# A mixer's depthwise convolution kept in PSUM, PE's units in two pairs of banks, and GpSimd's trailing means moved behind weight splits

## The chip, the cores and the metric

One core of one Trainium2 chip. The metric is the device time of one execution in microseconds (us). The kernel before took 3724.12 us (median of 3 runs, 3720.81 to 3726.64). Its profiled execution took 3723.6 us.

The engines are named as in the profile: PE (TensorE), DVE (VectorE), ACT (ScalarE), POOL (GpSimd), SP (SyncE, which issues the weights' transfers).

## What is computed

A first block (a mixer of gated delta rule and neighbourhood attention, then 16 experts), and behind it a second block of two layers over L = 528 tokens (16 meta tokens and 512) of 1024 features, all in float32. The change touches the second block's mixer alone:

```python
def token_mix(h, w_in, pool_w, pool_scale, conv_dw, conv_db, conv_ln_g, conv_ln_b, conv_pw, ret_gn_g, w_out):
    z = h @ w_in
    xp, ca, cg, q, k, v, g = jnp.split(z, splits, axis=-1)
    y_pool = pool_mixer(xp, pool_w, pool_scale)
    y_conv = conv_module(ca, cg, conv_dw, conv_db, conv_ln_g, conv_ln_b, conv_pw)
    y_ret = retention(q, k, v, g, ret_gn_g)
    return jnp.concatenate([y_pool, y_conv, y_ret], axis=-1) @ w_out

def conv_module(a, gate, w_dw, b_dw, ln_g, ln_b, w_pw):
    u = a * jax.nn.sigmoid(gate)
    y = lax.conv_general_dilated(u, w_dw[:, None, :], window_strides=(1,),
                                 padding=[(CONV_WIDTH - 1, 0)],
                                 dimension_numbers=('NWC', 'WIO', 'NWC'),
                                 feature_group_count=D_CONV) + b_dw
    y = jax.nn.silu(layer_norm(y, ln_g, ln_b))
    return y @ w_pw
```

The convolution has 31 taps over 256 channels (two tiles of 128). `pool_mixer` subtracts each token from trailing means over 2, 4, 8 and 16 tokens and multiplies by a matrix. `retention` rotates q and k (rope), forms decayed scores and values for 4 heads, normalises and gates them. Each layer is: a feed-forward network (FFN), a layer norm, this mixer, a layer norm, a second FFN, a layer norm.

## The kernel before

Features lie on the partitions, tokens along the row. A product of float32 is made of three passes in a rounded format: weights and activations are each split into a high and a low part, and `product` (L1852) adds w_hi·x_hi, w_hi·x_lo and w_lo·x_hi. **Weights come in pieces** of 1024 to 2048 columns: SP loads them, ACT rounds a piece into `w_hi` (`split_act`, L1837), POOL subtracts to get `w_lo` (`split_pool`, L1842), PE multiplies. There are two buffers of `w_hi` and `w_lo`, so the ACT half of piece i waits until PE is through with piece i-2 and POOL's half follows it. POOL takes the pieces strictly in the order of its program.

**The mixer's work on PE** is a list, `units`: xp (2, the pool mixer's input), ca and cg (2 each, value and gate of the convolution), q and k (4 each, by heads), v (10), g0, cm, g1, cq, g2, cb, g3 (gates of the retention with the convolution's layer norm between them: cm is the mean, cq the variance, cb the spread of the inverse root), pw (2), pool (2). A unit of ca, cg, q, k or g is 48 matmuls of 264 columns; one of v is 24 of 256. Pieces of the mixer hold the units so: piece 0 xp, 1 and 2 ca and cg, 3 to 6 one q and one k each, 7 and 8 five v each, 9 g0 and g1, 10 g2, 11 g3. PSUM has 8 banks, and unit w writes bank pair w modulo 4. Before it PE waits until the unit that had the pair (w-4) has been read (`taken`). ACT reads xp, cg, v, g, pw and pool, DVE reads ca, q, k and the rest.

**DVE** (`mix_dve`, L2268) multiplies ca by the sigmoid of cg (`gated`, L2286) into `u`, and then convolves: each of the 62 taps (2 tiles by 31) is one instruction over 528 columns, acc = u[shifted]·k + acc, with `u` and `acc` in SBUF. Tile 0's first ten taps stand between gated(0) and gated(1). Then come the eight units of q and k: for each, three instructions of rope that read PSUM (L2300 to L2302), followed by four taps. What is left of the taps (20) comes behind the last. The rope's sum is closed by POOL (L2262), and DVE's rope i waits for POOL's i-2.

```python
taps = [(0, w) for w in range(10)] + [(t, w + 10 - 10 * t) for w in range(21) for t in range(2)] + [(1, w) for w in range(21, CW)]
```

A drain stands before a tap of tile 0 and before each of the last ten. When a tile's 31 taps are done, `cv_sb` is raised, and PE's unit cm (L2046) reads `acc`.

**POOL** (`mix_pool`, L2237) takes piece 2, then for each of two tiles the trailing means of xp (L2248 to L2256) and one piece (3 and 4), then eight rope sums with a piece after each second one (5 to 8), then pieces 9, 10, 11 and those of the next FFN.

**ACT** (`mix_act`, L2174) issues the rounding of the next piece ahead of the first unit of a piece, and reads the units.

Of the kernel before, what the change touches and what calls it, by code (L numbers as in the profile page):

```python
# [1543 lines left out]
def second_block(E):  # L1544
# [398 lines left out]
    def ffn_dve(dve, l, w):  # L1943
        for g, (f0, nf) in enumerate(GROUPS):
# [22 lines left out]
            else:  # L1967
# [6 lines left out]
             [("pw", t, "a") for t in range(2)] + [("pool", t, "a") for t in range(2)])  # L1974
    place = {(kind, t): w for w, (kind, t, _) in enumerate(units)}

    in_pieces = ([[("xp", 0), ("xp", 1)]] + [[("ca", t), ("cg", t)] for t in range(2)] + [[("q", t), ("k", t)] for t in range(RH)] +
                 [[("v", 5 * j + t) for t in range(5)] for j in range(2)] + [[("g", 0), ("g", 1)], [("g", 2)], [("g", 3)]])
    where = {x: (i, j) for i, p in enumerate(in_pieces) for j, x in enumerate(p)}
# [12 lines left out]
    def taken(eng, l, kind, t):  # L1992
        e, n = done[place[kind, t]]
        (u_a if e == "a" else u_v).wait(eng, l, n)

    rope_s, kq_sb, yp_sb, cv_sb = Sig("rope_s", 8), Sig("kq_sb", 8), Sig("yp_sb", 2), Sig("cv_sb", 2)
    cc_sb, cq_sb, cr, ci, cn_sb, cs_sb = (Sig(x, n) for x, n in (
        ("cc_sb", 2), ("cq_sb", 2), ("cr", 1), ("ci", 1), ("cn_sb", 2), ("cs_sb", 2)))
    st_ps, st_sb, ro_ps, ro_sb = Sig("st_ps", 4 * RH), Sig("st_sb", 4 * RH), Sig("ro_ps", RH), Sig("ro_sb", RH)
    gm_ps, gc_sb, gq_sb, gv_ps, ge, gr, gi, gb_ps, gz, gy_sb = (Sig(x, RH) for x in (  # L2000
        "gm_ps", "gc_sb", "gq_sb", "gv_ps", "ge", "gr", "gi", "gb_ps", "gz", "gy_sb"))
# [21 lines left out]
    def mix_pe(pe, l):  # L2023
        for w, (kind, t, _) in enumerate(units):
            if w == 1:
                continue
            if w >= 4:
                taken(pe, l, *units[w - 4][:2])
            b = 2 * (w % 4)
            if (kind, t) in where:  # L2030
                i, j = where[kind, t]
                if j == 0:
                    wt = weights(pe, l, S_MIX + i)
            if kind == "xp":
                for last in first_two(pe, l, 0, [[x.rearrange("p (z k n) -> p z k n", z=2, k=DK)[:, z] for x in wt] for z in range(2)]):
                    last.then_inc(u_ps.sem, 1)
                continue
            if kind == "pool":
                yp_sb.wait(pe, l, t + 1)
                for h in range(2):  # L2040
                    last = nc.tensor.matmul(bank(b, h), pr["pool_w"][:, t * P:(t + 1) * P], halves(yp[:, t, :])[:, h, :], start=True, stop=True)
            elif kind == "cm":
                for x in range(2):
                    cv_sb.wait(pe, l, x + 1)
                    for h in range(2):
                        last = nc.tensor.matmul(bank(b, h), C["mean_c"], halves(acc[:, x, :])[:, h, :], start=(x == 0), stop=(x == 1))  # L2046
            elif kind == "cq":
                for x in range(2):
                    cq_sb.wait(pe, l, x + 1)
                    last = quads(b, 0, csq[:, x, :], x == 0, x == 1, "mean_c")  # L2050
            elif kind == "cb":
                ci.wait(pe, l, 1)
                last = spread_quads(b, mstat[2])
            elif kind == "pw":
                pw = pr["pw"].rearrange("p (k n) -> p k n", k=2)
                for x in range(2):
                    cs_sb.wait(pe, l, x + 1)
                    for h in range(2):
                        last = nc.tensor.matmul(bank(b, h), pw[:, x, t * P:(t + 1) * P], halves(acc[:, x, :])[:, h, :], start=(x == 0), stop=(x == 1))
            elif kind == "v":  # L2060
                s = TILES[t % 5][0]
                for k in range(DK):
                    for n, (wi, xi) in enumerate([(0, 0), (1, 0), (0, 1)]):
                        last = nc.tensor.matmul(PS[:, b, 0:256], (h_hi, h_lo)[xi][:, k, s:s + P],
                                                wt[wi].rearrange("p (k n) -> p k n", k=DK)[:, k, :],
                                                start=(k == 0 and n == 0), stop=(k == DK - 1 and n == 2))
            else:
                for k in range(DK):
                    at = j * D + k * P
                    last = product(b, [x[:, at:at + P] for x in wt], (h_hi[:, k, :], h_lo[:, k, :]), k == 0, k == DK - 1)  # L2070
            last.then_inc(u_ps.sem, 1)

        def scores(h):
            kq_sb.wait(pe, l, 2 * h + 2)
            for g, parts in enumerate(KEYS):
                if h:
                    st_sb.wait(pe, l, 4 * (h - 1) + g + 1)
                else:
                    taken(pe, l, *units[NU - 3 + g // 2][:2])
                for i, lo, hi, c in parts:  # L2080
                    s, n = TILES[i]
                    last = nc.tensor.matmul(PS[0:n, g, c:c + hi - lo], kT[:, h, s:s + n], qT[:, h, lo:hi], start=True, stop=True)
                last.then_inc(st_ps.sem, 1)
# [45 lines left out]
        scores(1)  # L2129
        values(0)  # L2130
        scores(2)
        taken(pe, l, "cb", 0)
        group_mean(0)
        values(1)
        group_var(0)
# [38 lines left out]
    def mix_act(act, l):  # L2174
# [62 lines left out]
    def mix_pool(pool, l):  # L2237
        nc.gpsimd.tensor_tensor(xp[:, 0, 0:16], C["cnt"][:, 0:16], C["cnt"][:, 0:16], ALU.subtract)
        nc.gpsimd.memset(xp[:, 1, 0:16], 0.0)
        nc.gpsimd.memset(u[:, :, 0:CW - 1], 0.0)  # L2240
        nc.gpsimd.drain().then_inc(xz_sb.sem, 1)
        split_pool(pool, l, S_MIX + 2)
        for t in range(2):
            taken(pool, l, "xp", t)
            x, s, r = xp[:, t, :], win2[:, 0, :], win2[:, 1, :]
            src, sh, dst = x, 1, s
            for step in range(2 if t == 0 else 4):
                nc.gpsimd.tensor_tensor(dst[:, 2 * sh:], src[:, 2 * sh:], src[:, sh:544 - sh], ALU.add)  # L2248
                nc.gpsimd.drain()
                src, sh, dst = dst, 2 * sh, (r if dst is s else s)  # L2250
            for half, y in ((0, s), (1, r)):
                a, b = half * 64, half * 64 + 64
                nc.gpsimd.tensor_tensor(yp[a:b, t, 0:16], y[a:b, 16:32], C["cnt"][a:b, 16 * t:16 * t + 16], ALU.mult)
                nc.gpsimd.tensor_scalar(yp[a:b, t, 16:], y[a:b, 32:544], C["win"][a:b, t:t + 1], None, ALU.mult)
            nc.gpsimd.drain()
            nc.gpsimd.tensor_tensor(yp[:, t, :], yp[:, t, :], x[:, 16:544], ALU.subtract)  # L2256
            nc.gpsimd.drain().then_inc(yp_sb.sem, 1)
            split_pool(pool, l, S_MIX + 3 + t)
        for i in range(8):
            rope_s.wait(pool, l, i + 1)  # L2260
            x = (kT if i % 2 else qT)[:, i // 2, :]
            nc.gpsimd.tensor_tensor(x, x, ropet[:, i % 2, :], ALU.add).then_inc(kq_sb.sem, 1)  # L2262
            if i % 2:
                split_pool(pool, l, S_MIX + 5 + i // 2)
        for i in range(S_MIX + 9, S_FFN2 + 2):
            split_pool(pool, l, i)

    def mix_dve(dve, l):  # L2268
        taps = [(0, w) for w in range(10)] + [(t, w + 10 - 10 * t) for w in range(21) for t in range(2)] + [(1, w) for w in range(21, CW)]

        def convolve(n):
            for _ in range(n):
                t, w = taps.pop(0)
                if t == 0 or w >= 21:
                    nc.vector.drain()
                k = pr["dw"][:, t * CW + w:t * CW + w + 1]
                if w == 0:
                    last = nc.vector.tensor_scalar(acc[:, t, :], u[:, t, w:w + L], k, pr["conv_db"][:, t:t + 1], ALU.mult, ALU.add)
                else:
                    last = nc.vector.scalar_tensor_tensor(acc[:, t, :], u[:, t, w:w + L], k, acc[:, t, :], ALU.mult, ALU.add)  # L2280
                if w == CW - 1:
                    last.then_inc(cv_sb.sem, 1)

        def gated(t):
            taken(dve, l, "cg", t)
            nc.vector.tensor_tensor(halves(u[:, t, CW - 1:]), halves(acc[:, t, :]), bank(2 * (place["ca", t] % 4)), ALU.mult).then_inc(u_v.sem, 1)  # L2286

        par_in.wait(dve, l, 16)
        xz_sb.wait(dve, l, 1)
# [2 lines left out]
        gated(1)  # L2292
        for i in range(8):
            kind = "qk"[i % 2]
            b = 2 * (place[kind, i // 2] % 4)
            made(dve, l, kind, i // 2)
            if i >= 2:
                kq_sb.wait(dve, l, i - 1)
# [5 lines left out]
            nc.vector.drain().then_inc(u_v.sem, 1)  # L2304
            convolve(4)
        convolve(len(taps))
        b = 2 * (place["cm", 0] % 4)
        nc.vector.drain()
        made(dve, l, "cm", 0)
        for t in range(2):  # L2310
            nc.vector.tensor_tensor(halves(acc[:, t, :]), halves(acc[:, t, :]), bank(b), ALU.subtract).then_inc(cc_sb.sem, 1)
        nc.vector.drain().then_inc(u_v.sem, 1)
        made(dve, l, "cq", 0)
        nc.vector.tensor_scalar(mstat[2], PS[:, 2 * (place["cq", 0] % 4), 0:QN], LN_EPS, None, ALU.add).then_inc(u_v.sem, 1)
        cr.wait(dve, l, 1)
        nc.vector.reciprocal(mstat[2], mstat[2]).then_inc(ci.sem, 1)
        made(dve, l, "cb", 0)
        b = 2 * (place["cb", 0] % 4)
        for t in range(2):
            nc.vector.tensor_tensor(halves(acc[:, t, :]), halves(acc[:, t, :]), bank(b), ALU.mult).then_inc(cn_sb.sem, 1)  # L2320
        nc.vector.drain().then_inc(u_v.sem, 1)
# [294 lines left out]
```

## Time and profile before

| | before |
|---|---|
| runs | 3724.12 us median (3720.81 to 3726.64) |
| profiled execution | 3723.6 us, span 3721.8 us |
| PE busy | 3382.1 us (91%) |
| DVE busy | 1130.5 us (30%) |
| POOL busy | 1004.6 us (27%) |
| ACT busy | 838.6 us (23%) |
| granted TensorE clock, mean | 0.96 |

The span runs from the first to the last instruction that the profiler recorded. Busy shares are means over stages of different kinds. The two mixers lie near 1941 to 2205 us and 3023 to 3288 us of the span. A granted clock of 1.00 is the upper level (2.4 GHz), 0.50 the lower (1.2 GHz).

### The profile page before, as it was taken

How to read it: one execution, taken by the hardware profiler on the slowest of the kernel's cores; microseconds unless marked ns; L12 is line 12 of the kernel's file. 1: busy time of each engine (PE TensorE's matmuls, PEld its weight loads, DVE VectorE, ACT ScalarE, POOL GpSimd, SP SyncE). 2: the span in 40 equal slices, each digit the busy share in tenths (PEclk: the TensorE clock that was granted, in tenths of full speed). 3: DMA queues.
4: the chain of work that ended last, by engine and by line, in shares of the span. 5: the costliest groups of instructions: out<-in, count | busy, mean ns of one | idle time of the engine just before them, and what ended most of it. 6: DMA issues, size and time to landing. Idle time of an engine off the chain costs nothing. (4 is left out here: it accounts for less than half of the span.)

```text
span 3721.8 us, 54577 instructions
## 1 busy us (share of the span) xinstructions
PE 3382.1 (91%) x23608; PEld 2789.9 (75%) x23608; DVE 1130.5 (30%) x1619; ACT 838.6 (23%) x1071; POOL 1004.6 (27%) x419
## 2 busy tenths in 40 slices
PE   3889989978699998699998999999999998999997
PEld 0446568974343433699988779999999988789996
DVE  1224655562321212311138431111211158331113
ACT  1023321111100000422241232222422241142223
POOL 0002134410100000333336114333433354034333
PEclk7899999998799999899999999999999999999998
DMA  8332100002599998222221112222222211022221
GB/s 336 127 113 72 68 1 1 1 1 91 229 380 400 405 381 353 75 91 91 80 74 69 46 69 91 91 86 80 74 91 93 84 69 69 27 87 91 91 80 41
DMA packets 37146, 446.62 MB, mean 120 GB/s; under 512 B 5568, under 2 KB 6336, under 8 KB 10816
## 3 DMA queue, kind: packets, MB, share of 16 engines
q1 hardware_dynamic: 34112, 432.25, 29.7%
q10 hardware_dynamic: 2816, 11.16, 0.8%
q8 instruction: 174, 2.85, 0.3%
q14 instruction: 44, 0.36, 0.0%
HBM read 441.30 MB, written 2.10 MB: 119 GB/s over the span
## 5 line engine op out<-in xcount | busy, mean ns | idle before, releaser
L1842 POOL TENSOR_TENSOR w_lo<-low,w_hi 128x2048 fp32r<-128x2048 f32 (+2 forms) x162 | 713.9, 4407 | 1825.3 <-ACT w_hi L1837 1824.3
L1852 PE MATMUL PS<-h_hi,w_hi 128*128 128x264 f32 x3136 | 644.7, 287 | 13.3 <-POOL w_lo L1842 13.3
L1852 PE MATMUL PS<-h_lo,w_hi 128*128 128x264 f32 x3136 | 640.2, 286 | 0.0
L1852 PE MATMUL PS<-h_hi,w_lo 128*128 128x264 f32 x3136 | 636.4, 284 | 0.0
L1852 PEld LDWEIGHTS PS<-h_hi,w_hi 128*128 128x128 f32 x3136 | 487.8, 190 | 15.8 <-POOL w_lo L1842 10.5
L1852 PEld LDWEIGHTS PS<-h_lo,w_hi 128*128 128x128 f32 x3136 | 490.3, 189 | 0.0
L1852 PEld LDWEIGHTS PS<-h_hi,w_lo 128*128 128x128 f32 x3136 | 490.2, 190 | 0.0
L1837 ACT ACTIVATE w_hi<-low 128x2048 fp32r<-128x2048 f32 (+2 forms) x162 | 295.1, 1821 | 471.7 <-PE PS L1852 469.5
L1951 DVE TENSOR_TENSOR low<-low,PS 128x528 f32<-128x528 f32 x84 | 59.2, 705 | 800.6 <-PE PS L1852 763.2
L1852 PE MATMUL PS<-g_hi,w_hi 128*128 128x264 f32 (+1 forms) x1408 | 295.8, 291 | 3.5 <-ACT low L1930 3.5
L1852 PE MATMUL PS<-g_lo,w_hi 128*128 128x264 f32 (+1 forms) x1408 | 286.1, 285 | 0.0
L1852 PE MATMUL PS<-g_hi,w_lo 128*128 128x264 f32 (+1 forms) x1408 | 284.4, 283 | 0.0
L1405 PE MATMUL PS<-arena 128*64 128x512 f32 x1024 | 226.8, 595 | 19.1 <-DVE arena L1450 12.1
L1852 PEld LDWEIGHTS PS<-g_hi,w_hi 128*128 128x128 f32 (+1 forms) x1408 | 216.4, 188 | 18.1 <-issue 6.6
L1852 PEld LDWEIGHTS PS<-g_hi,w_lo 128*128 128x128 f32 (+1 forms) x1408 | 218.7, 188 | 0.0
L1852 PEld LDWEIGHTS PS<-g_lo,w_hi 128*128 128x128 f32 (+1 forms) x1408 | 218.6, 188 | 0.0
L1961 DVE SCALAR_TENSOR_TENSOR high<-PS,high 128x528 f32<-128x528 f32 x96 | 68.0, 708 | 445.4 <-PE PS L1852 445.4
L1405 PEld LDWEIGHTS PS<-arena 128*64 128x64 f32 x1024 | 81.6, 137 | 158.7 <-issue 158.7
L2280 DVE SCALAR_TENSOR_TENSOR low<-high,low 128x528 f32<-128x528 f32 x120 | 175.3, 1488 | 9.7 <-issue 4.9
L1933 ACT ACTIVATE g_hi<-low 128x528 fp32r<-128x528 f32 x88 | 56.9, 646 | 483.5 <-DVE low L1951 480.4
L1421 PE MATMUL PS<-arena 128*64 128x512 f32 x512 | 113.4, 594 | 11.2 <-DMA arena<-wts_dram 9.9
L1440 ACT ACTIVATE arena<-PS 64x512 f32<-64x512 f32 x32 | 18.9, 591 | 443.8 <-PE PS L1405 443.8
(346 smaller groups left out, 4439.2 us busy)
## 6 DMA issues: line engine op xcount, KB each, us to landing
arena<-wts_dram SPq DMA_DIRECT2D x117, 2048.0 KB, 14.6
low<-wts_dram SPq DMA_DIRECT2D x70, 2048.0 KB, 7.7
low<-wts_dram SPq DMA_DIRECT2D x12, 1536.0 KB, 6.4
arena<-na_bias_dram SPq DMA_DIRECT2D x16, 768.0 KB, 4.2
arena<-b_mod_dram ACTq DMA_DIRECT2D x1, 3072.0 KB, 33.7
arena<-x_dram ACTq DMA_DIRECT2D x1, 2048.0 KB, 71.4
arena<-x_dram SPq DMA_DIRECT2D x1, 2048.0 KB, 8.0
low<-wts_dram SPq DMA_DIRECT2D x2, 1024.0 KB, 5.1
```

Source lines behind the costliest of these rows:

```text
L1405: last = nc.tensor.matmul(PS[a:b, 2 + 2 * j + half, :], xe[:, k, j * CAP:(j + 1) * CAP], w[:, k, :], start=(k == 0), stop=(k == DK - 1))
L1421: last = nc.tensor.matmul(PS[a:b, 2 + half, :], hidT[:, k, j * CAP:(j + 1) * CAP], w[j][:, k, :], start=(k == 0), stop=(k == DK - 1))
L1440: nc.scalar.activation(hs[c:d, half * 512:(half + 1) * 512], PS[a:b, 2 + 2 * j + half, :], ACT.Silu).then_inc(hs_sb, 1)
L1837: nc.scalar.activation(hi, raw, ACT.Copy).then_inc(w_h.sem, 1)
L1842: nc.gpsimd.tensor_tensor(lo, raw, hi.bitcast(F32), ALU.subtract).then_inc(w_l.sem, 1)
L1852: mm = nc.tensor.matmul(bank(b, h), w[wi], halves(x[xi])[:, h, :], start=(first and i == 0), stop=(last and i == 2))
L1933: nc.scalar.activation(g_hi[r, f - f0, :], gs[r, f % 2, :], ACT.Copy).then_inc(gh_sb.sem, 1)
L1951: nc.vector.tensor_tensor(halves(x), halves(x), bank(4 * (f % 2) + 2), ALU.mult).then_inc(g_sb.sem, 1)
L1961: nc.vector.scalar_tensor_tensor(halves(res[:, m, :]), bank(2 * (m % apart)), 0.5, halves(res[:, m, :]), ALU.mult, ALU.add).then_inc(dn_sb ...
L2280: last = nc.vector.scalar_tensor_tensor(acc[:, t, :], u[:, t, w:w + L], k, acc[:, t, :], ALU.mult, ALU.add)
```

## The change

1. The convolution's accumulator moves from SBUF (`acc`) to PSUM: tile 0 in banks 4 and 5, tile 1 in banks 6 and 7. The taps read `u` from SBUF and the accumulator from PSUM and write PSUM. Their number and order stay.
2. ACT copies the finished accumulators to `acc` (2 instructions of 528 columns), ahead of its reading of g0, and raises the new semaphore `ac_sb`, for which PE waits before cm, g1 and cq.
3. PE's units take their bank pair from a table, `double`. The units of q, k and v alternate between pairs 1 and 0. A unit waits for the one that last had its pair (`bank_before`): for q, k and v that is the second before it, in place of the fourth.
4. POOL takes pieces 2, 3 and 4 first, then the rope sums with pieces 5 to 8, then the trailing means of each tile with pieces 9 and 10, then 11 and the rest.

```diff
+    double = [0, 1, 2, 3, 0, 3] + [1, 0] * 9 + [1, 0, 2, 3, 1, 0, 2, 3, 0, 1, 2]
+    def unit_bank(kind, t):
+        return 2 * double[place[kind, t]]
+    def bank_before(w):
+        return next((units[x][:2] for x in range(w - 1, -1, -1) if double[x] == double[w]), None)
+    def conv_acc(t):
+        return PS[:, 4 + 2 * t:6 + 2 * t, 0:LH]
...
     def mix_pe(pe, l):
-            if w >= 4:
-                taken(pe, l, *units[w - 4][:2])
-            b = 2 * (w % 4)
+            if bank_before(w):
+                taken(pe, l, *bank_before(w))
+            if (kind, t) in (("g", 1), ("cq", 0)):
+                ac_sb.wait(pe, l, 2)
+            b = unit_bank(kind, t)
...
             elif kind == "cm":
                 for x in range(2):
-                    cv_sb.wait(pe, l, x + 1)
+                    ac_sb.wait(pe, l, x + 1)
...
     def mix_act(act, l):
+            if (kind, t) == ("g", 0):
+                for x in range(2):
+                    cv_sb.wait(act, l, x + 1)
+                    nc.scalar.activation(halves(acc[:, x, :]), conv_acc(x), ACT.Copy).then_inc(ac_sb.sem, 1)
...
     def mix_pool(pool, l):
-        split_pool(pool, l, S_MIX + 2)
+        for i in range(2, 5):
+            split_pool(pool, l, S_MIX + i)
+        for i in range(8):
+            rope_s.wait(pool, l, i + 1)
+            x = (kT if i % 2 else qT)[:, i // 2, :]
+            nc.gpsimd.tensor_tensor(x, x, ropet[:, i % 2, :], ALU.add).then_inc(kq_sb.sem, 1)
+            if i % 2:
+                split_pool(pool, l, S_MIX + 5 + i // 2)
         for t in range(2):
             taken(pool, l, "xp", t)
...
-            split_pool(pool, l, S_MIX + 3 + t)
...
+            split_pool(pool, l, S_MIX + 9 + t)
+        for i in range(S_MIX + 11, S_FFN2 + 2):
             split_pool(pool, l, i)
...
     def mix_dve(dve, l):
+                src = halves(u[:, t, w:w + L])
                 if w == 0:
-                    last = nc.vector.tensor_scalar(acc[:, t, :], u[:, t, w:w + L], k, pr["conv_db"][:, t:t + 1], ALU.mult, ALU.add)
+                    last = nc.vector.tensor_scalar(conv_acc(t), src, k, pr["conv_db"][:, t:t + 1], ALU.mult, ALU.add)
                 else:
-                    last = nc.vector.scalar_tensor_tensor(acc[:, t, :], u[:, t, w:w + L], k, acc[:, t, :], ALU.mult, ALU.add)
+                    last = nc.vector.scalar_tensor_tensor(conv_acc(t), src, k, conv_acc(t), ALU.mult, ALU.add)
```

POOL's program from the mixer's piece 3 on, before (L1842 is a piece's low part, L2248 to L2256 the means of tile 0, L2262 a rope sum):

```order
L1842 TENSOR_TENSOR w_lo<-low,w_hi 128x2048
L1644 ISA
L2248 TENSOR_TENSOR low<-low 128x542
L2248 TENSOR_TENSOR low<-low 128x540
L2253 TENSOR_TENSOR low<-low,high 64x16
L2254 TENSOR_SCALAR low<-low,high 64x512
L2253 TENSOR_TENSOR low<-low,high 64x16
L2254 TENSOR_SCALAR low<-low,high 64x512
L2256 TENSOR_TENSOR low<-low 128x528
L1644 REGISTER_ALU
L1842 TENSOR_TENSOR w_lo<-low,w_hi 128x2048
```

And of the change, the same place (the first three rows of L1842 are pieces 2, 3 and 4; L2266 is the rope sum):

```order
L1842 TENSOR_TENSOR w_lo<-low,w_hi 128x2048
L1644 REGISTER_ALU
L1842 TENSOR_TENSOR w_lo<-low,w_hi 128x2048
L1644 REGISTER_ALU
L1842 TENSOR_TENSOR w_lo<-low,w_hi 128x2048
L1644 ISA
L2266 TENSOR_TENSOR high<-high,low 128x528
L1644 REGISTER_ALU
L2266 TENSOR_TENSOR high<-high,low 128x528
L1644 REGISTER_ALU
L1842 TENSOR_TENSOR w_lo<-low,w_hi 128x2048
```

Between pieces 2 and 3, and between 3 and 4, nothing of the means is left; they stand behind piece 8.

ACT's program of the change where g0 is read (L1837 is the rounding of piece 10, L2202 the new copies out of PSUM, L2222 the reading of g0, L2206 the squares for cq):

```order
L1837 ACTIVATE w_hi<-low 128x1024 [waits l_sb1,arrived0]
L1644 ISA
L2202 ACTIVATE low<-PS 128x528 [waits w_sb1]
L1644 REGISTER_ALU
L2202 ACTIVATE low<-PS 128x528 [waits w_sb1]
L1644 REGISTER_ALU
L2222 ACT_TABLE_LOAD
L2222 ACTIVATE high<-PS 128x528 [waits l_sb1]
L2206 ACTIVATE low<-low 128x528 [waits lt_sb1] x2
```

The copies stand behind the rounding of piece 10 and ahead of g0.

## Rows read from the trace of the kernel before

**Rows 1.** Waits of PE, 1945 to 2100 us (layer 1): total us, times, longest.
```profile
PE PS L2064 <- POOL w_lo L1842: 5.0, 2, 4.6
PE PS L1852 <- POOL w_lo L1842: 4.8, 2, 4.6
PE PS L2046 <- DVE low L2280: 3.6, 1, 3.6
```

**Rows 2.** Waits of PE, 3027 to 3185 us (layer 2).
```profile
PE PS L2064 <- POOL w_lo L1842: 5.2, 2, 4.8
```

**Rows 3.** Timeline of PE, layer 1: start, us, instructions [idle before, releaser].
```profile
1989.94 0.81 PE L1852 MATMUL PS<-h_hi,w_hi 128*128 128x264 f32 x2 [4.55 <-POOL w_lo L1842]
```

**Rows 4.** PE by stretches: window, its us, busy (matmuls), granted clock, DMA share, GB/s.
```profile
1961.30:1972.97 11.67, 11.67 (x98) 1.00 0.39 160
...
1989.94:1996.16 6.22, 6.22 (x28) 0.50 0.84 300
...
2032.62:2037.12 4.50, 4.50 (x21) 0.50 0.01 4
...
2074.38:2078.08 3.70, 3.70 (x14) 0.54 0.00 0
...
3072.37:3078.19 5.82, 5.82 (x26) 0.50 0.88 310
3115.07:3119.15 4.08, 4.08 (x19) 0.50 0.00 0
3156.74:3160.11 3.37, 3.37 (x11) 0.50 0.02 5
```

**Rows 5.** Timeline of POOL, layer 1.
```profile
1959.72 2.32 POOL L2248 TENSOR_TENSOR low<-low 128x542 f32<-128x542 f32 x2
...
1968.59 4.79 POOL L1842 TENSOR_TENSOR w_lo<-low,w_hi 128x2048 fp32r<-128x2048 f32 x1 [0.24 <-issue]
1973.33 6.31 POOL L2248 TENSOR_TENSOR low<-low 128x542 f32<-128x542 f32 x4
...
1985.19 4.70 POOL L1842 TENSOR_TENSOR w_lo<-low,w_hi 128x2048 fp32r<-128x2048 f32 x1 [0.24 <-issue]
...
2026.31 1.32 POOL L2262 TENSOR_TENSOR high<-high,low 128x528 f32<-128x528 f32 x1 [4.94 <-DVEq L2303]
2027.59 4.97 POOL L1842 TENSOR_TENSOR w_lo<-low,w_hi 128x2048 fp32r<-128x2048 f32 x1
```

**Rows 6.** Timeline of DVE, layer 1.
```profile
2000.94 0.70 DVE L2300 TENSOR_TENSOR high<-PS,high 128x528 f32<-128x528 f32 x1
...
2003.33 3.95 DVE L2280 SCALAR_TENSOR_TENSOR low<-high,low 128x528 f32<-128x528 f32 x4 [0.25 <-issue]
2007.20 0.70 DVE L2300 TENSOR_TENSOR high<-PS,high 128x528 f32<-128x528 f32 x1
...
2026.46 8.20 DVE L2280 SCALAR_TENSOR_TENSOR low<-high,low 128x528 f32<-128x528 f32 x4 [0.25 <-issue]
...
2056.48 5.32 DVE L2280 SCALAR_TENSOR_TENSOR low<-high,low 128x528 f32<-128x528 f32 x7
```

**Rows 7.** Single lines, whole span: duration in ns, least, median, most.
```profile
L2280 DVE SCALAR_TENSOR_TENSOR low<-high,low x120: 755/769/5109, 1963.6 to 3155.9; 128x528 f32<-128x528 f32 x120
...
L2300 DVE TENSOR_TENSOR high<-PS,high x16: 696/701/708, 1979.6 to 3123.3; 128x528 f32<-128x528 f32 x16
...
L1961 DVE SCALAR_TENSOR_TENSOR high<-PS,high x96: 707/708/711, 1636.6 to 3689.1; 128x528 f32<-128x528 f32 x96
...
L339 DVE SCALAR_TENSOR_TENSOR arena<-arena x6: 1278/1279/1285, 107.6 to 120.0; 128x1024 f32<-128x1024 f32 x6
```

**Rows 8.** Timeline of ACT, layer 1: piece 4 rounded; g0 read out of PSUM.
```profile
1973.67 1.90 ACT L1837 ACTIVATE w_hi<-low 128x2048 fp32r<-128x2048 f32 x1
...
2069.90 0.61 ACT L2203 ACTIVATE high<-PS 128x528 f32<-128x528 f32 x1 [3.21 <-PE PS L1852]
```

More of the change, by code:

```diff
@@ L1975, in second_block @@
     place = {(kind, t): w for w, (kind, t, _) in enumerate(units)}
+    double = [0, 1, 2, 3, 0, 3] + [1, 0] * 9 + [1, 0, 2, 3, 1, 0, 2, 3, 0, 1, 2]
+    assert len(double) == len(units)
+    def unit_bank(kind, t):
[4 more added lines that the diff above has]
+        return PS[:, 4 + 2 * t:6 + 2 * t, 0:LH]
     in_pieces = ([[("xp", 0), ("xp", 1)]] + [[("ca", t), ("cg", t)] for t in range(2)] + [[("q", t), ("k", t)] for t in range(RH)] +
@@ L1996, in second_block @@
     rope_s, kq_sb, yp_sb, cv_sb = Sig("rope_s", 8), Sig("kq_sb", 8), Sig("yp_sb", 2), Sig("cv_sb", 2)
-    cc_sb, cq_sb, cr, ci, cn_sb, cs_sb = (Sig(x, n) for x, n in (
-        ("cc_sb", 2), ("cq_sb", 2), ("cr", 1), ("ci", 1), ("cn_sb", 2), ("cs_sb", 2)))
+    ac_sb, cc_sb, cq_sb, cr, ci, cn_sb, cs_sb = (Sig(x, n) for x, n in (
+        ("ac_sb", 2), ("cc_sb", 2), ("cq_sb", 2), ("cr", 1), ("ci", 1), ("cn_sb", 2), ("cs_sb", 2)))
     st_ps, st_sb, ro_ps, ro_sb = Sig("st_ps", 4 * RH), Sig("st_sb", 4 * RH), Sig("ro_ps", RH), Sig("ro_sb", RH)
@@ L2078, in scores @@
                 else:
-                    taken(pe, l, *units[NU - 3 + g // 2][:2])
+                    taken(pe, l, *(("pw", 1), ("pool", 0))[g // 2])
                 for i, lo, hi, c in parts:
@@ L2131, in mix_pe @@
         scores(2)
-        taken(pe, l, "cb", 0)
+        taken(pe, l, "pw", 0)
         group_mean(0)
@@ L2182, in mix_act @@
                     split_act(act, l, S_MIX + i + 1)
-            b = 2 * (w % 4)
+            b = unit_bank(kind, t)
+            if (kind, t) == ("g", 0):
+                for x in range(2):
+                    cv_sb.wait(act, l, x + 1)
+                    nc.scalar.activation(halves(acc[:, x, :]), conv_acc(x), ACT.Copy).then_inc(ac_sb.sem, 1)
             if kind == "cm":
@@ L2257, in mix_pool @@
             nc.gpsimd.drain().then_inc(yp_sb.sem, 1)
-            split_pool(pool, l, S_MIX + 3 + t)
[L2259 to L2265, printed above, removed]
+            split_pool(pool, l, S_MIX + 9 + t)
+        for i in range(S_MIX + 11, S_FFN2 + 2):
             split_pool(pool, l, i)
@@ L2285, in gated @@
             taken(dve, l, "cg", t)
-            nc.vector.tensor_tensor(halves(u[:, t, CW - 1:]), halves(acc[:, t, :]), bank(2 * (place["ca", t] % 4)), ALU.mult).then_inc(u_v.sem, 1)
+            nc.vector.tensor_tensor(halves(u[:, t, CW - 1:]), halves(acc[:, t, :]), bank(unit_bank("ca", t)), ALU.mult).then_inc(u_v.sem, 1)
         par_in.wait(dve, l, 16)
@@ L2294, in mix_dve @@
             kind = "qk"[i % 2]
-            b = 2 * (place[kind, i // 2] % 4)
+            b = unit_bank(kind, i // 2)
             made(dve, l, kind, i // 2)
@@ L2306, in mix_dve @@
         convolve(len(taps))
-        b = 2 * (place["cm", 0] % 4)
+        b = unit_bank("cm", 0)
         nc.vector.drain()
@@ L2313, in mix_dve @@
         made(dve, l, "cq", 0)
-        nc.vector.tensor_scalar(mstat[2], PS[:, 2 * (place["cq", 0] % 4), 0:QN], LN_EPS, None, ALU.add).then_inc(u_v.sem, 1)
+        nc.vector.tensor_scalar(mstat[2], PS[:, unit_bank("cq", 0), 0:QN], LN_EPS, None, ALU.add).then_inc(u_v.sem, 1)
         cr.wait(dve, l, 1)
@@ L2317, in mix_dve @@
         made(dve, l, "cb", 0)
-        b = 2 * (place["cb", 0] % 4)
+        b = unit_bank("cb", 0)
         for t in range(2):
```

## The prediction

> **What bounds the kernel now.** I read the page first: PE is busy almost everywhere, 91% of the span, at a mean granted clock of 0.96. Then PE's waits in each mixer. There are five: two at weight pieces of q and k (4.8 us), two at those of v (5.0), one at cm (3.6), 13.4 us in layer 1 [rows 1] and 13.6 in layer 2, where the v pieces cost 5.2 [rows 2] and the other two rows read as in layer 1. The timeline shows the one at piece 4, 4.55 us [rows 3]; the other long ones are at piece 7 (4.6) and before the second half of cm (3.6), and two of 0.3 to 0.4 us, at pieces 3 and 8, make up the rest. Last the stretches behind the three long waits: PE had stood idle, and the granted clock in them is 0.50, the lower level. A matmul there comes every 6.22/28 = 0.222 us, at full clock every 11.67/98 = 0.119 [rows 4]. So each us spent at the lower level loses 1 - 0.119/0.222 = 0.46 us.
>
> Why PE waits. POOL finished pieces 3 and 4 late, since it had formed the means first: the means of tile 1 begin at 1973.33, and piece 4 is begun only at 1985.19, while PE had come to it at 1985.4 [rows 3, 5]. Piece 7 was begun at 2027.59, behind the sixth rope sum, which waited 4.94 us for DVE [rows 5]. And DVE was behind because its taps collide with POOL: a tap has a median of 769 ns and a maximum of 5109 [rows 7]. The four taps from 2026.46 took 8.20 us, with POOL's 4.97 us subtraction over them; the four from 2003.33, where POOL had one rope sum of 1.32 us, took 3.95 [rows 5, 6]; seven with POOL idle nearly throughout took 5.32, 0.76 each [rows 6]. Rope starts lie 6.26 us apart where the four taps took 3.95 (2000.94 to 2007.20), so 10.5 where they took 8.20; the two come in turn [rows 6], 8.4 us a unit on average, while PE needs 5.84 (half of 11.67). Four bank pairs let PE run ahead; POOL's late pieces, and at the end cm, return the delay.
>
> **The change, part by part.**
>
> *Taps into PSUM.* 62 per layer, as before; no instruction is removed. No row before has DVE writing PSUM, so the price is bounded. Below: 708 ns, the same kind of instruction with PSUM read, SBUF written and an immediate in place of the column scalar [rows 7]. Above, leaving POOL out of it: 1279 ns, that of 1024 columns in place of 528 [rows 7], as though reading and writing a bank took turns. I take 0.77, since PSUM as a source makes no visible difference (rope at 701 ns). And does it free the taps from POOL? Rope instructions have one SBUF tensor and one in PSUM, and all 16 of L2300 lie between 696 and 708 ns while the taps between them go up to 5109 [rows 7]. A tap will have the same: `u` in SBUF, the sum in PSUM.
>
> A DVE round is then rope with its drains, 2003.33 - 2000.94 = 2.39 us [rows 6], and 4 taps of 0.76, 3.05: 5.44 us, less than PE's 5.84. DVE is no longer behind, and finds each unit of q and k at its end. The table of cycle costs in the Trainium skill ("VectorE: DVE Perf Modes", section on the TRN2 errata) speaks against this: it gives PSUM sources 120 cycles of fixed cost where SBUF sources have 58. By it a tap would be 65 ns longer, an estimate from that page, and the round 5.70, which is still below PE's, so that the sum would be the same but the margin 0.14 in place of 0.40. The rows disagree with it: 701 and 708 ns with a PSUM source.
>
> *Two bank pairs for q, k and v.* k0 waits for gated(1): PE ends cg1 at 1973.1, ACT's sigmoid and DVE's multiply are over near 1974.6, and k0 begins only at 1979.0. From then each unit needs the rope of the one but last, which is done 2.4 us into the 5.84 of the unit between. The narrow place is v1, which needs the rope of k3: k3 ends near 2019.8, its rope near 2022.3, and v0 ends at 2022.65 (a v unit: 24 matmuls of 0.119, 2.86 us). The margin is 0.3 us, I cost it at nothing. ACT reads a whole unit of g in 0.61 [rows 8], so v and g are never late.
>
> *POOL's order.* Piece 4's low part can begin near 1975.6, behind PE's end of piece 2 (1973) and ACT's rounding (1.90 us from 1973.67 [rows 8]), and is ready near 1980.3, where PE wants it at 1984.8; piece 3's likewise, one piece earlier. From then per piece: the second rope sum ends 3.6 us after its k unit was made, and the subtraction of 4.6 to 5.0 ends 8.6 us after; PE wants it at 11.67. Margin 3. Piece 7 is ready near 2016.5, PE wants it at 2019.8. So the waits at pieces 3, 4, 7 and 8 go. Behind piece 8 (near 2028.5) come the means of tile 0, 8.9 us before (1959.72 to 1968.59 [rows 5]), piece 9 until 2042 (wanted at 2048), the means of tile 1, 11.9 us (1973.33 to 1985.19), until 2054, and piece 10 (half the columns, so 2.4 us) until 2057, wanted near 2062. The means themselves are wanted only by the units pool, after 2070. Their cost is thus hidden by v and g0; without that cover up to 20.8 us would lie open.
>
> *cm.* DVE has 20 taps left after its last round, 42 being done by 2025.5, and ends near 2042. ACT's two copies, 1.2 us by the 0.61 of g0 [rows 8], stand behind v9 and the rounding of piece 10, and end near 2050.7; PE comes to cm near 2054. So the 3.6 us wait goes as well. What queues behind the new wait: on ACT the reading of g0 and all after it, on PE cm and g1, and neither is due before 2054.
>
> *The clock.* With no long idle there is nothing ahead of the three stretches at 0.50. Layer 1: (6.22 + 4.50 + 3.70) · 0.46 = 6.6 us; layer 2: (5.82 + 4.08 + 3.37) · 0.46 = 6.1 [rows 4].
>
> **Sum.** 13.4 + 13.6 + 6.6 + 6.1 = 39.7 us off the profiled 3723.6: 3683.9. The median of the runs lies 0.5 above the profiled execution, so 3684.5 for the median. What is late next is nothing in this stage: PE is then the bound from the first to the last unit.
>
> **The rivals.**
>
> *A round too long for two banks.* If a tap comes every 0.95 us in place of 0.76 the round is 6.19, 0.35 over PE's, 2.5 us behind after seven rounds, less the 0.3: 2.2 us at v1, and a stretch at the low clock behind it, 3.4 · 0.46 = 1.6. Two layers: 7.6, so 3692. Against it the equal times of PSUM and SBUF sources, for it that the drain must await a write into PSUM, which no row shows.
>
> *Reading and writing one bank takes turns.* At 1.28 us a tap the round is 7.5, 1.67 over, 11.7 us after seven, less 0.3, and the low clock after some stalls, 1 to 2 us: 13 per layer, so 3710. The last 20 taps would then take 27 us, to about 2063, just in time for cm. The Trainium skill ("PSUM — Partial Sum Buffer", section on bank collisions) calls a bank in a partition a RAM of its own that two engines may not use in one cycle; it says nothing of one engine that reads and writes it, and no row here shows that.
>
> *Slower: taps still blocked by POOL.* Each tap also takes a column scalar from SBUF, which rope does not, so the rows of rope don't wholly decide. If the block stays, DVE's rounds stay at 8.4 us on average, k3's rope ends near 2043 as before, and v1, which formerly went ahead, now waits for it: v ends at 2069, g0 at 2075. Meanwhile DVE's 24 taps (19 us) and POOL's two means with pieces 8 and 9 (about 30) exclude each other: the taps end near 2043 + 49 = 2092 in place of 2074.3, and cm and g0's reading wait for them. 18 us a layer: 3760. The point from which the whole change costs time is a DVE round of about 8.3 us (39.7/2 = 19.9 us in eight rounds, over 5.84).
>
> *The change doesn't reach the end.* PE gains the time and loses it at a later transfer. In the mixers PE's waits name no DMA [rows 1, 2], so little speaks for it: 3724.
>
> **How the numbers follow.** Forecast 0.71, long round 0.11, turns 0.06, blocked 0.07, no effect 0.05 (with gains below 0.2%). A measurement of this kernel can tell about 0.2%, 7.4 us, from no change. Faster: 0.71 + 0.11 + 0.06 = 0.88; within: 0.05; slower: 0.07. The range goes from 3680 (means or sums shorter, spread of the runs 3 us down) to 3708, over the long round and toward the taps in turns; it leaves out the blocked and the no-effect case and some of the turns, about 0.16.
>
> **What would show it.** Right: L2301, the tap, with a maximum near its median of 0.7 to 0.8 us, no wait of PE for w_lo, for DVE or for ac_sb in the mixers, PE's granted clock at 1.00 from ca0 to the end of v, rope starts 5.84 us apart, and each mixer about 20 us shorter. Wrong: a tap over 0.86 us including drain (then v1 waits for DVE), maxima of 5 us (blocked), waits of PE for w_lo at piece 10 or ahead of pool (means too late), or ACT's copies begun after g0 was made. It would also be wrong if the lower clock came although PE doesn't wait.

## The result and the profile after

The changed kernel took 3680.21 us (median of 4 runs, 3678.80 to 3683.80), the kernel before, run beside it, 3725.38 (3720.81 to 3729.83): a ratio of 0.9875, 95% interval 0.9849 to 0.9902. That is 45 us less by the medians where 39.7 were forecast, and 0.9875 of the 3724.12 us stated for the kernel before is 3677.6, under the forecast's low end of 3680 (the measured median itself lies 0.2 above it). The direction and the mechanism were right, the size 3 to 6 us short. A second timing gave 3679.28 (3677.57 to 3680.34) against 3723.13, ratio 0.9880 (0.9864 to 0.9897).

Both mixers, from the first matmul of ca0 to the first of the next FFN's long run, as stretches of PE: window, its us, busy (matmuls), granted clock, DMA share, GB/s. Before:

```profile
1949.61:2227.77 278.16, 260.06 (x1763) 0.96 0.17 61
3032.04:3310.11 278.07, 258.85 (x1762) 0.96 0.17 61
```

After:

```profile
1952.43:2209.25 256.82, 251.53 (x1762) 0.99 0.18 66
3013.98:3270.81 256.83, 251.55 (x1763) 0.99 0.18 66
```

21.34 and 21.24 us less, 42.6 in all, with the same matmuls: 1760 start in each stretch (the counts above take in some at the edges). Asked for its waits between 1952.5 and 2180 us, PE of the changed kernel names none where [rows 1] named three groups, and its granted clock is 1.00 from ca0 until the first products of the next FFN, at the end of the stretch:

```profile
1952.43:2197.60 245.17, 240.04 (x1684) 1.00 0.17 62
```

The taps of both layers, by their line over the whole span (ns, least, median, most):

```profile
L2301 DVE SCALAR_TENSOR_TENSOR PS<-high,PS x120: 764/772/775, 1966.7 to 3105.4; 128x528 f32<-128x528 f32 x120
L2299 DVE TENSOR_SCALAR PS<-high x4: 823/828/831, 1965.8 to 3046.5; 128x528 f32<-128x528 f32 x4
```

The median is that of [rows 7] (769), but the most is 775 in place of 5109. DVE's timeline of a round, and of the last taps:

```profile
1987.67 0.71 DVE L2321 TENSOR_TENSOR high<-PS,high 128x528 f32<-128x528 f32 x1 [0.40 <-PE PS L1852]
...
1990.08 2.98 DVE L2301 SCALAR_TENSOR_TENSOR PS<-high,PS 128x528 f32<-128x528 f32 x4 [0.26 <-issue]
1993.61 0.71 DVE L2321 TENSOR_TENSOR high<-PS,high 128x528 f32<-128x528 f32 x1 [0.55 <-PE PS L1852]
...
1999.44 0.71 DVE L2321 TENSOR_TENSOR high<-PS,high 128x528 f32<-128x528 f32 x1 [0.45 <-PE PS L1852]
...
2037.90 6.70 DVE L2301 SCALAR_TENSOR_TENSOR PS<-high,PS 128x528 f32<-128x528 f32 x8 [0.43 <-issue]
2058.64 1.32 DVE L2332 TENSOR_TENSOR low<-low,PS 128x528 f32<-128x528 f32 x2 [14.04 <-PE PS L2061]
```

The four taps took 2.98 us, and from the second round on DVE waits 0.4 to 0.55 us for PE; the rope starts lie 5.83 to 5.94 apart. The taps end at 2044.6, 12 us ahead of cm. POOL's timeline while those taps ran:

```profile
1991.20 4.62 POOL L1842 TENSOR_TENSOR w_lo<-low,w_hi 128x2048 fp32r<-128x2048 f32 x1
...
2026.34 4.61 POOL L1842 TENSOR_TENSOR w_lo<-low,w_hi 128x2048 fp32r<-128x2048 f32 x1
2030.91 2.32 POOL L2274 TENSOR_TENSOR low<-low 128x542 f32<-128x542 f32 x2
...
2043.71 5.00 POOL L2274 TENSOR_TENSOR low<-low 128x542 f32<-128x542 f32 x4
...
2054.26 2.40 POOL L1842 TENSOR_TENSOR w_lo<-low,w_hi 128x1024 fp32r<-128x1024 f32 x1 [0.24 <-issue]
```

POOL gains too: a piece of 2048 columns takes 4.62 us where [rows 5] has 4.70 to 4.97, and four steps of the means 5.00 in place of 6.31. Piece 10 is ready at 2056.7, about 8 us before g2 asks for it. ACT around the copies:

```profile
2051.31 1.05 ACT L1837 ACTIVATE w_hi<-low 128x1024 fp32r<-128x1024 f32 x1
2052.26 1.10 ACT L2202 ACTIVATE low<-PS 128x528 f32<-128x528 f32 x2
```

They end at 2053.4; PE comes to cm at 2056.66 and does its eight matmuls without a stop. So the two copies delay nothing:

```profile
2056.66 1.94 PE L2061 MATMUL PS<-low,high 128*128 128x264 f32 x8
```

### The profile page after: what moved, and what is told of

Read it like the earlier page. It is cut to its first block and busy times, and to the rows that moved or that the text cites. A ratio compares the mean times of both kernels' runs of the same rounds, so it can differ in the third digit from the quotient of the medians.

```text
span 3682.0 us, 54585 instructions
## 1 busy us (share of the span) xinstructions
PE 3369.2 (92%) x23608; PEld 2780.1 (76%) x23608; DVE 1045.9 (28%) x1619; ACT 840.6 (23%) x1075; POOL 995.3 (27%) x419
## 5 line engine op out<-in xcount | busy, mean ns | idle before, releaser
L1842 POOL TENSOR_TENSOR w_lo<-low,w_hi 128x2048 fp32r<-128x2048 f32 (+2 forms) x162 | 710.1, 4383 | 1814.1 <-ACT w_hi L1837 1813.6
L1837 ACT ACTIVATE w_hi<-low 128x2048 fp32r<-128x2048 f32 (+2 forms) x162 | 295.1, 1821 | 455.4 <-PE PS L1852 453.3
L525 POOL TENSOR_SCALAR arena<-arena 128x768 f32<-128x768 f32 x32 | 28.5, 905 | 294.6 <-DVE arena L505 294.6
```

Source lines behind the costliest of these rows:

```text
L525: nc.gpsimd.tensor_scalar(p, p, rr[:, x:x + 1], 1.0, ALU.mult, ALU.mult).then_inc(sc_nrm, 1)
L1837: nc.scalar.activation(hi, raw, ACT.Copy).then_inc(w_h.sem, 1)
L1842: nc.gpsimd.tensor_tensor(lo, raw, hi.bitcast(F32), ALU.subtract).then_inc(w_l.sem, 1)
```

## The experiments

Four questions: which part of the change brings the gain; what a stop of PE costs; whether two bank pairs are a limit; and what is scatter. The letters of the theories are explained in each expectation. Each kernel ran beside the kernel before. "The stretch" is that from ca0 to the next FFN, 278.16 and 278.07 us before, 256.82 and 256.83 in the changed kernel. Its 1760 matmuls stand in the same order in every kernel here, so a "lag" can be given as well: how much later than in the changed kernel a matmul starts, both counted from ca0. A stop is a place where the lag grows, and nothing that happens later mixes in.

### The changed kernel again

No edit.

> The changed kernel once more, with more rounds. Theory F (a stop of PE costs more than its listed idle time and the low clock: the pipeline has to drain and fill, about 0.35 us a stop): the stretch from ca0 to the next FFN is 21.3 us shorter in each layer, so 42.6 us in all, near 3681 to 3682 where the kernel before has 3724. Rival N (the forecast's sum of 39.7 us was right and the rest of the measured gain is scatter of the runs): near 3684.5, and the stretch is 20 us shorter.

3679.28 us, 43.9 less than before. The stretch, in its layer 1:

```profile
1946.61:2203.43 256.82, 252.33 (x1762) 0.99 0.18 66
```

It is the same to 0.01 us (0.02 in layer 2), while the two profiled executions of this one kernel have spans of 3682.0 and 3675.8. Of those 6.2 us 5.8 arose before ca0 of layer 1 (1952.43 against 1946.61), in stages that the change does not touch. The medians could not decide, since the intervals of both ratios hold 39.7 as well as 42.6. The stretch decides for the size that theory F gives: 42.6, not 39.7 or 40.

What is left of the 43.9 and 45 can be looked for outside the stretches, in the twelve profiled executions on record (the kernel before, the changed kernel twice, nine variants). Ahead of ca0 they took 1946.6 to 1952.4 us, without order by kernel, and between the mixers 803.3 to 804.7. Behind the second stretch the four with the sum in SBUF took 411.7 to 411.8 and the eight with it in PSUM 410.9 to 411.2. So about 0.6 us of the gain lies at the very end of the kernel, for a reason that is not shown. What then remains, 0.7 to 2 us, is less than the scatter of the first stage alone.

### The sum back in SBUF

```diff
     def conv_acc(t):
-        return PS[:, 4 + 2 * t:6 + 2 * t, 0:LH]
+        return halves(acc[:, t, :])
...
-            if (kind, t) in (("g", 1), ("cq", 0)):
-                ac_sb.wait(pe, l, 2)
...
-            if (kind, t) == ("g", 0):
-                for x in range(2):
-                    cv_sb.wait(act, l, x + 1)
-                    nc.scalar.activation(halves(acc[:, x, :]), conv_acc(x), ACT.Copy).then_inc(ac_sb.sem, 1)
```

(cm waits for `cv_sb` again.)

> The changed kernel with the convolution's sum back in SBUF, without ACT's copies: two bank pairs and POOL's new order stay. Theory P (the taps with two SBUF tensors are held up by POOL, and the move to PSUM is what frees them): taps up to 5 us long, DVE's rounds of 8.4 us on average, PE waits at v1 or before for DVE and at cm for the taps: 3745 to 3765. Rival Q (the order of POOL and the banks bring the gain, the move to PSUM is idle): within 5 us of the changed kernel, 3680 to 3687.

3727.01 us, ratio to before 1.0011 (1.0002 to 1.0021): 47.7 us slower than the changed kernel at 3679.28. The taps, and two rounds of DVE with POOL's piece in the first:

```profile
L2295 DVE SCALAR_TENSOR_TENSOR low<-high,low x120: 752/769/5114, 1961.7 to 3156.4; 128x528 f32<-128x528 f32 x120
```

```profile
2002.50 8.30 DVE L2295 SCALAR_TENSOR_TENSOR low<-high,low 128x528 f32<-128x528 f32 x4 [0.26 <-issue]
...
2013.11 3.93 DVE L2295 SCALAR_TENSOR_TENSOR low<-high,low 128x528 f32<-128x528 f32 x4 [0.26 <-issue]
...
2036.20 27.99 DVE L2295 SCALAR_TENSOR_TENSOR low<-high,low 128x528 f32<-128x528 f32 x16 [0.26 <-issue]
2064.61 9.88 DVE L2295 SCALAR_TENSOR_TENSOR low<-high,low 128x528 f32<-128x528 f32 x8 [0.43 <-issue]
```

Waits of PE, layer 1:

```profile
PE PS L1852 <- DVEq L2319: 6.2, 2, 4.6
PE PS L2077 <- DVEq L2319: 5.7, 2, 3.1
PE PS L2059 <- DVE low L2295: 3.3, 1, 3.3
```

PE waits for the rope of the second unit before, in q, k and v, and at cm. Theory P holds in kind: without the move to PSUM the other two parts are worth nothing. Its time was 18 us or more too long. Two things were wrong. The rope of k3 began at 2033.8, 86.0 us behind ca0, where it begins 91.2 behind in the kernel before: the first round from rope to rope, which the means drew out to 10.8 us there, took 6.1 here. And the last 24 taps took 38 us beside POOL, not 49 as if one engine had always stood while the other worked.

### POOL's old order with the sum in PSUM

`mix_pool` as in the kernel before (means of tile 0 between pieces 2 and 3, of tile 1 between 3 and 4), all else as changed:

```diff
-        for i in range(2, 5):
-            split_pool(pool, l, S_MIX + i)
+        split_pool(pool, l, S_MIX + 2)
...
-            split_pool(pool, l, S_MIX + 9 + t)
+            split_pool(pool, l, S_MIX + 3 + t)
```

> The changed kernel with POOL's old order: sum in PSUM, two bank pairs, but the trailing means between pieces 2, 3 and 4. Theory P: POOL is not held up by DVE any more, so the means of tile 1 take 10.6 us in place of 11.9, and PE waits only at piece 4, for about 2.9 us, plus 0.35 for the pipeline and about 3 us at the low clock: 6 us a layer, 3690 to 3697, DVE on time from piece 5 on. Rival Q: all the old waits at pieces 4 and 7 come back, 9.4 us and two stretches at the low clock a layer: 3707 or more.

3687.18 us: 7.9 slower than the changed kernel, and faster than expected. PE waits at piece 4 alone, for 2.27 us in layer 1 and 2.53 in layer 2, and the stretch grows by 2.71 and 4.30 (259.53 and 261.13). The lag behind the stop is 2.54 and 4.32; the other 0.17 us of layer 1 arose at the end of the stretch, in the first products of the next FFN. In layer 1 the clock stays at 1.00, in layer 2 there are 3.4 us at 0.50; the expected 3 us at the low clock in each layer were too many. Stretches behind the two stops, all engines: window, its us, then busy us of PE, PEld, DVE, ACT and POOL, the clock, DMA share and GB/s:

```profile
1985.30:1990.00 4.70, 4.70 (x38) 4.70 (x39) 2.90 (x4) 0.00 (x0) 4.70 (x3) 1.00 0.81 268
3049.07:3053.00 3.93, 3.93 (x19) 3.93 (x20) 2.81 (x4) 0.00 (x0) 3.93 (x3) 0.57 0.78 242
```

### POOL's new order alone

The kernel before with `mix_pool` of the change.

```diff
-        split_pool(pool, l, S_MIX + 2)
+        for i in range(2, 5):
+            split_pool(pool, l, S_MIX + i)
...
-            split_pool(pool, l, S_MIX + 3 + t)
+            split_pool(pool, l, S_MIX + 9 + t)
```

> The kernel before with POOL's new order alone: sum in SBUF, four bank pairs. Theory P: the wait at piece 4 goes (4.8 us and about 3 us of low clock), but the taps are still held up, now by the means too, which stand beside the last taps, and cm waits 10 to 16 us: a gain of 8 and a loss of 8 to 14 a layer, 3720 to 3740, no gain. Rival Q: 3680 to 3690, since the pieces are on time.

3729.01 us, ratio to before 1.0013 (1.0003 to 1.0022). Waits of PE, layer 1:

```profile
PE PS L2046 <- DVE low L2281: 10.1, 1, 10.1
PE PS L2064 <- POOL w_lo L1842: 3.7, 2, 3.3
PE PS L1852 <- POOL w_lo L1842: 3.0, 2, 2.4
```

As theory P says: the means stand beside the last taps in place of the first (the last 24 take 38.3 us), and cm waits 10.1 us. The gain at piece 4 is spent there.

### The bank pairs alone

The kernel before with the table `double` and its `bank_before`, sum in SBUF, old order:

```diff
-            if w >= 4:
-                taken(pe, l, *units[w - 4][:2])
-            b = 2 * (w % 4)
+            if bank_before(w):
+                taken(pe, l, *bank_before(w))
+            b = unit_bank(kind, t)
```

> The kernel before with the table of bank pairs alone: sum in SBUF, POOL's old order, no copies on ACT. Theory R (a DVE round over PE's unit costs where PE can't run ahead): DVE's rounds stay 8.4 us, k3's rope ends near 2043 as in the kernel before, v1 waits for it (before it started near 2035.5), and the wait at cm goes since DVE's taps end at 2074 while PE comes later: 3 to 6 us a layer slower than before, 3730 to 3736. Rival S (the bank pairs don't matter, as the sum in SBUF with the new order gave 3727 with two pairs and 3729 with four): 3720 to 3727.

3722.94 us against 3722.76, ratio 1.0004 (0.9994 to 1.0013): no change, where theory R gave 3730 to 3736. PE now waits for DVE in q, k and v:

```profile
PE PS L2077 <- DVEq L2318: 4.9, 2, 3.4
...
PE PS L1852 <- DVEq L2318: 4.7, 2, 4.6
```

and no longer at cm: the stretch is 277.66 us, 0.5 less. As expected v1 started at 2043.16, but the waits at piece 7 and at cm went in exchange: the running ahead of four pairs in the kernel before only led to waits further on. The even result has a second cause, which the expectation left out. PE's listed waits in layer 1 are 14.4 us against 13.4, but the granted clock was low for less time behind them:

```profile
1989.85:1992.82 2.97, 2.97 (x13) 0.50 0.70 177
2020.14:2023.54 3.40, 3.40 (x15) 0.50 0.72 304
2036.99:2040.61 3.62, 3.62 (x17) 0.53 0.00 0
```

That is 10.0 us in place of the 14.4 of the kernel before [rows 4], worth 2.0 us at 0.46. So while the taps are blocked, two pairs cost about 1.5 us a layer (an estimate: those 2.0 less the 0.5 by which the stretch is shorter), and a shorter low clock hid it.

### Five and six taps a round

```diff
-            convolve(4)
+            convolve(5)
```

> The changed kernel with five taps behind each rope in place of four (62 in all as before, so 12 are left for the end). DVE's round becomes 5.40 + 0.75 = 6.15 us, 0.31 over PE's 5.84. Theory R (with two bank pairs PE can't run ahead, so a DVE round over PE's unit costs its excess, gathered at v1): 2.2 us behind after seven rounds, less 0.3 of slack: PE waits 1.9 us at v1, 2.3 us a layer with drain and fill, up to 3.9 if the clock falls: 3684 to 3687. Rival S (there is room in the pieces and in the 20 taps that are moved forward, DVE's rounds don't set anything): 3680, no wait of PE.

3687.70 us, 0.7 above the expected range. PE waits once in the mixer, at v1, 2.22 us in layer 1 and 2.24 in layer 2, and the stretch grows by 2.88 and 4.40. The lag behind the stop is 2.50 without a low clock and 4.03 with 3.4 us of it; the other 0.4 us of each layer arose at the end of the stretch.

And with `convolve(6)`:

> The same with six taps behind each rope, which leaves 4. Round 6.9 us, 1.06 over PE's. Theory R: 7.4 us behind at k3, less 0.3: PE's waits begin two to three units before v and sum to 7.1 us a layer, plus 0.4 for each stop and 1 to 3 us of low clock: 9 to 12 us a layer, 3697 to 3703. Rival S: 3680.

3699.27 us, inside the expected 3697 to 3703. PE's waits, layer 1:

```profile
PE PS L2079 <- DVEq L2325: 4.6, 2, 3.7
PE PS L1852 <- DVEq L2325: 1.6, 2, 0.9
```

6.2 us listed, the stretch longer by 10.57 and 8.87. Here theory R holds: where PE is otherwise never held up, a DVE round over 5.84 us costs, and the changed kernel has 0.4 to 0.5 us of room a round. The prediction's rival of the long round was thus real, only the taps were not that slow.

### Stops of PE of a chosen length

```diff
         for i in range(2, 5):
+            if i == 4:
+                _, raw, _, _ = piece(S_MIX + i)
+                w_h.wait(pool, l, S_MIX + i + 1)
+                scratch = win2.rearrange("p a n -> p (a n)")
+                for c in [1080, 1080]:
+                    nc.gpsimd.tensor_tensor(scratch[:, 0:c], raw[:, 0:c], raw[:, 0:c], ALU.add)
+                    nc.gpsimd.drain()
             split_pool(pool, l, S_MIX + i)
```

> The changed kernel with two extra additions of 1080 columns on POOL (into the means' scratch) ahead of its part of piece 4, about 5.1 us, of which about 4.3 us are slack: PE waits at piece 4 for 0.8 to 1.1 us in each layer. Theory F: no low clock behind so short a stop, and the stretch from ca0 to the next FFN grows by the listed idle plus 0.35 to 0.45 us, so 1.2 to 1.5 us a layer, 3681 to 3683 in all. Rival N (a stop costs its listed idle and what the clock takes, no more): 0.8 to 1.1 us a layer.

3679.67 us, and no wait of PE: two additions took 4.12 us, not 5.1, and POOL's slack swallowed them (stretch 256.87 and 256.88). That slack is 4.4 us: piece 4 is ready at 1983.1 in the changed kernel, and PE comes to it near 1987.5. The run says nothing on F or N; it shows that 4 us of extra POOL work there are free.

With the list `[1080, 1080, 1080, 500]`:

> The same with four additions, 3740 columns, about 8.9 us: PE waits at piece 4 for 4.3 to 4.8 us in each layer, as long as in the kernel before, in an otherwise unchanged mixer. Theory F: idle 4.5, 0.4 for drain and fill, and a stretch at the lower clock of 3.4 to 6.8 us that loses 0.46 us per us (1.6 to 2.9): 6.5 to 7.8 us a layer, 3693 to 3696 in all. Rival N: 4.5 + 1.6 to 2.9 = 6.1 to 7.4. If the low clock came with the mixer whatever PE does, its stretches would not depend on the stop and the cost would be 4.5 alone.

3689.88 us, 3 under the expectation: the stops were 3.01 us in both layers, shorter than meant. PE's timeline at each:

```profile
1986.27 0.41 PE L1852 MATMUL PS<-h_hi,w_lo 128*128 128x264 f32 x2
1989.68 0.51 PE L1852 MATMUL PS<-h_hi,w_hi 128*128 128x264 f32 x2 [3.01 <-POOL w_lo L1842]
1990.03 0.41 PE L1852 MATMUL PS<-h_lo,w_hi 128*128 128x264 f32 x2
...
3053.85 0.81 PE L1852 MATMUL PS<-h_hi,w_hi 128*128 128x264 f32 x2 [3.01 <-POOL w_lo L1842]
3054.46 0.64 PE L1852 MATMUL PS<-h_lo,w_hi 128*128 128x264 f32 x2
```

and its clock behind them:

```profile
1989.68:1993.00 3.32, 3.32 (x27) 1.00 0.70 212
3053.85:3056.80 2.95, 2.95 (x13) 0.50 0.71 178
```

The stretch grew by 3.29 us in layer 1, where the clock stayed: 3.01 listed and 0.28 more. This decides against rival N, since no clock is in it. The timeline shows the 0.28: the last pair of matmuls starts at 1986.27 and the next pair at 1989.68, 3.41 us in place of the usual 0.24, so 3.17 lost; the listed idle begins only at the end of the last one. The first pair then takes 0.35 us to the next in place of 0.24. In layer 2 the stretch grew by 4.60: 1.31 more, for 2.97 us at the low clock, where the 0.46 per us of the prediction gives 1.37. The pairs above, 0.44 us apart at the low clock and 0.24 at the full one, give 0.45.

With `[1080, 1080, 1080, 1080, 320]`:

> The changed kernel with 4640 columns of extra additions on POOL ahead of its part of piece 4, so that PE waits there 4.4 to 4.8 us a layer, as at piece 4 of the kernel before (4.55 us). The run with 3740 columns had waits of 3.01 us, which lengthened the stretch from ca0 to the next FFN by 3.29 us in layer 1 without a low clock and by 4.60 in layer 2 with 3.4 us of low clock. Theory F: idle 4.6 + 0.3 to 0.4 for drain and fill + 3.4 to 6.8 us at the low clock, 1.3 to 2.9: 6.2 to 7.9 us a layer, 3692 to 3696. Rival N (listed idle and clock alone): 0.3 to 0.4 less for each stop. The clock of before would be reproduced if the low stretch lasts 6.8 us.

3692.78 us. Stops of 4.79 and 4.80 us, the stretch longer by 6.53 and 6.59; PE ran at 0.50 for 3.25 us behind the first and 3.4 behind the second:

```profile
1988.25:1991.50 3.25, 3.25 (x15) 0.50 0.72 192
```

In layer 1 4.79 + 3.25 · 0.46 = 6.28, and 0.25 more. (The expectation's ranges for F and N overlap, so the total alone would not have told them apart.) The 6.22 us at the low clock that the kernel before shows behind a stop of 4.55 [rows 3, 4] were not reproduced.

### The parts side by side

| sum of the taps | bank pairs | POOL's order | us |
|---|---|---|---|
| SBUF | four | old (the kernel before) | 3723.1 |
| SBUF | four | new | 3729.0 |
| SBUF | two | old | 3722.9 |
| SBUF | two | new | 3727.0 |
| PSUM | two | old | 3687.2 |
| PSUM | two | new (the change) | 3679.3 |

The sum in PSUM is worth 36 us under the old order and 48 under the new. The new order costs 4 to 6 us without it and brings 8 with it. Two bank pairs, which the sum in PSUM needs, show no cost in the totals of either order (but see the clock above). PSUM with four pairs for the units can't be had: the two accumulators take four of the eight banks.

## Why the prediction was right in kind and short in size

**Waits and their releasers.** Right. All five waits a layer went. Where the time came from, by the starts of PE's units relative to ca0 in layer 1: 12.9 us by the start of v, 15.8 by g0, 20.3 by g1, 21.35 by cq, and from there to the layer norm's end both kernels run alike. The stage is rid of its stops: from ca0 to the layer norm's end the granted clock was 1.00.

**The tap's price.** Right: 0.77 was taken between 708 and 1279 ns, 772 measured. The Trainium skill's table ("VectorE: DVE Perf Modes", TRN2 errata), by which a PSUM source costs 62 cycles more, does not describe these taps: 772 ns with a PSUM source and destination, 769 with both in SBUF. Only the first tap of a tile is dearer, 828 ns where the kernel before has 554 to 686, four times in the whole kernel.

**POOL and DVE.** Right: the block is gone although each tap also takes its column scalar from SBUF, the point that the rows before left open. The Trainium skill ("SBUF — State Buffer", Who interferes with whom) says that a DVE instruction with at most one SBUF input does not contend with GpSimd, outside the modes that use both ports; the 772 ns agree, also beside the means.

**Two bank pairs.** Right: DVE's room of 0.4 a round was 0.40 to 0.55, and v1 did not wait. The rival of the long round was priced at 3.8 us a layer for taps of 0.95 us; five taps a round, likewise 0.3 over PE's unit, cost 2.5 us without a low clock and 4.0 with it.

**The step that failed** is the term of the waits in the sum, "13.4 + 13.6". It took the listed idle time as the whole of what a stop costs beside the clock. The stops that the experiments made cost 0.22 to 0.28 us more each, since the listed time starts at the end of the last matmul and the first pair behind a stop comes slower. The kernel before shows it at its own five stops, by the lag (layer 1, us):

| stop before | listed | with 0.46 per us of low clock | lag gained |
|---|---|---|---|
| piece 3 | 0.30 | 0.30 | 0.58 |
| piece 4 | 4.55 | 7.41 | 7.60 |
| piece 7 | 4.59 | 6.66 | 6.85 |
| piece 8 | 0.40 | 0.40 | 0.70 |
| second half of cm | 3.62 | 5.32 | 5.48 |
| sum | 13.46 | 20.09 | 21.21 |

The two short stops, which no low clock follows, cost 0.28 and 0.30 more than listed. The three long ones cost 0.16 to 0.19 more, and 0.20 to 0.25 with 0.45 for the low clock. Short delays between the stops make up the last 0.1. The stretches give the same: 21.34 against 13.4 + 6.6 = 20.0 in layer 1, 21.24 against 13.6 + 6.1 = 19.7 in layer 2. Together 2.9 us, and the forecast would have been 3681.6.

**The range** failed in its own way: the missing 2.9 us alone lead to 3681.6, still inside it. Its low end of 3680 left 4.5 us under the sum, of which 3 were meant for scatter of the runs, and those 2.9 us used most of it. The 1.3 to 2.6 us from 42.6 to the 43.9 and 45 measured are the 0.6 at the kernel's end and scatter; the stage ahead of ca0 varies by 5.8 us between executions.

**A rival's price.** The rival of taps still blocked by POOL, at 3760, stood for a state that the sum back in SBUF made: 3727. So it was priced 33 us too high, with the two errors named there. The prediction's own point of no gain, a DVE round of 8.3 us, was closer: there the rounds took 8.1 us on average.

## What to carry to other kernels

A DVE accumulation with two SBUF tensors that runs beside POOL can be freed by keeping its sum in PSUM: here the instruction costs the same and is no longer held up, and POOL speeds up too. Look first who is late behind whom: reordering POOL cost 6 us alone and brought 8 once the tap and the piece no longer blocked each other, and a deeper set of buffers only moved the wait. When stops of PE are removed, count for each the listed idle, about 0.3 us for the end and the restart that the listing leaves out, and the low clock behind it, and leave room for scatter on both sides of the range.

## What the runs showed of the hardware that was not expected

- The same stop of 3.01 us was followed by 3.0 us of work at the lower clock in one layer and by none in the other of one execution; 2.27 us had none, 2.53 had 3.4, 4.79 had 3.25, and the same stop of 4.55 us at piece 4 had 6.2 in the kernel before [rows 4] and 2.97 with the bank pairs alone, where its lag was 6.2 in place of 7.6 us. So in this range the idle time listed for a stop did not alone decide whether and how long the clock fell.
- DVE reads and writes the same PSUM banks in one instruction at its usual rate: 772 ns for 528 columns, and 2.98 us for four.
- With DVE's second SBUF tensor gone, POOL's own additions became shorter: 4.62 us for 2048 columns against 4.70 to 5.08, and 5.00 us for four steps of the means against 6.31.
- The mixer's stretch repeats to 0.01 and 0.02 us between two executions of one kernel whose spans differ by 6 us, so a stretch of the trace can settle a term of 1 us that the medians can't. Its end, with the first products of the next FFN, added up to 0.65 us in some of the other kernels; the lag ahead of them is free of that.
